# RWKV state of eight decoding samples: four token steps on GpSimd replaced by one chunk of four tokens with TensorE products

## The chip, the core and the metric

The kernel runs on one core of one Trainium2 chip. The metric is the device time of one launch in microseconds; lower is better. Its engines are called PE (TensorE), DVE (VectorE), ACT (ScalarE), POOL (GpSimd) and SP (SyncE) below, as in the profile.

## The reference, cut to what matters

The kernel computes one inference step of a one-layer hybrid decoder: 512 prompt tokens and 8 samples of 4 new tokens each. A combined projection feeds an RWKV-7 mixer and a sparse attention; the two are merged and projected back. The change concerns the RWKV mixer for the samples alone: 8 samples x 16 heads = 128 independent states of 64 x 64, each advanced over 4 tokens.

```python
def step(S, inp):                       # S: (b, h, i, j); i the value index, j the key index
    r_t, k_t, v_t, kk_t, a_t, w_t = inp
    sa = jnp.einsum('bhij,bhj->bhi', S, kk_t)
    S = (S * w_t[:, :, None, :] - sa[..., None] * (kk_t * a_t)[:, :, None, :]
         + v_t[..., None] * k_t[:, :, None, :])
    return S, jnp.einsum('bhij,bhj->bhi', S, r_t)
...
S, o = lax.scan(step, S0.astype(f32), xs)      # 4 steps for a sample
mean = jnp.mean(o, axis=-1, keepdims=True)
var = jnp.mean(jnp.square(o - mean), axis=-1, keepdims=True)
o = (o - mean) * lax.rsqrt(var + GN_EPS) * gn_w.reshape(H, N) + gn_b.reshape(H, N)
o = o + jnp.sum(r * k * r_k, axis=-1, keepdims=True) * v
o = o.reshape(B, T, A_WIDTH) * jax.nn.silu(g.astype(f32))
```

Outputs that depend on it are the sample rows of y and the new state `s_rwkv`.

## The kernel before, in words

**Stages.** The kernel is a sequence of stages: the RWKV mixer of the prompt, the compression of the cached rows, the prompt's attention (`attend_prompt`, here called the prompt stage), the samples' attention, and the output projection. An engine enters a stage when all have ended the one before (`T.enter`, `T.end`).

**The background projection.** All stages up to the samples' attention share one long piece of PE work, the combined projection. Its weights come in halves h of 128 x 1024 numbers: SP loads a half (`w_raw`, L155, two buffers; it waits until `w_lo` of the half two before is made), ACT copies it to a rounded `w_hi` (L161), another engine subtracts to make `w_lo` (L168), and PE multiplies it in four pieces of 12 matmuls each (L200). In the prompt stage `w_lo` is made by POOL; in the others by DVE. Two halves form a chunk, which ACT evacuates (L208). Each engine runs pieces, copies and evacuations in order between its other work, up to a number that a planned place gives (`background(upto)`). The prompt stage holds 12 chunks, 96 pieces. The first 16 stand ahead of PE's entry, the last 12 behind all attention work, and 68 are spread over the rest. At the start of the stage PE and ACT first do some of this background work and then wait to enter.

**The prompt stage.** There are 16 rows (4 groups x 4 heads), each of 4 query tiles t of 128 queries, so 64 units u = 4w + t. PE's work for a unit: two score products S0 and S1 of the next unit (L1919), the transposes T0 and T1 (L1928), and the value product O of the unit before (L1939, L1941). At t = 1 comes the compressed score product C of the next row (L1906), at t = 3 its transpose CT (L1913). DVE reduces scores while it copies them out (`maxes`, L1822; `row_maxes`, L1830), copies T1 (L1870) and combines the outputs (`outs`, L1847 to L1852); ACT takes exponentials (L1756, L1763) and copies T0 (L1796) and CT (L1771). Four PSUM banks serve these jobs in turn, in the order in which `prompt_jobs` lists them: job k takes the bank of job k - 4 and waits until that is copied out (`held`, `taken`).

Ahead of the first row's exponentials ACT has to do all background work up to piece 16: `w_hi` of the halves h0+4, h0+5 and h0+6 and the evacuation of the first two chunks, where h0 is the stage's first half. CT of row 0 waits for these exponentials, and the loop over the units stands behind CT.

**The samples' state.** `rwkv_samples` runs inside the prompt stage. The 128 states lie one to a partition, 64 x 64 numbers each. DVE and ACT make the vectors (`dve_before`, `act_before`); POOL then does `pool_steps`:

```python
for t in range(DEC_T):
    link(tt(prod[:, :, :], S[:, :, :], last_dim(kk, t), ALU.mult))
    tt(S[:, :, :], S[:, :, :], last_dim(w, t), ALU.mult)
    link(row_sums(sa[:, :]))
```

and so on: five products and two sums of 128 x 4096 numbers for a token and two trees of sums (`row_sums`, L1476 and L1478). After each linked instruction `between()` is called, which puts a `w_lo` on POOL where its count is due. POOL's order at the start of the stage is: load the samples' data, `w_lo` of h0+2, wait for the vectors, the first product of 128 x 4096 (L1480), `w_lo` of h0+3 and h0+4.

DVE does five more small operations for the samples in the loop, among them three products of two SBUF tensors (L1521, L1522 and L1524, in units 8, 9 and 11). At the end of the stage DVE and ACT normalise the outputs (`dve_after`, `act_after`), and SP stores the new state (2 MB, L1443) and the outputs (L1445) and waits for both to land before the stage ends (`store`).

Of the kernel before, what the change touches and what calls it, by code (L numbers as in the profile page):

```python
# [19 lines left out]
F32 = mybir.dt.float32  # L20
# [1389 lines left out]
def rwkv_samples(nc, A, ctx):  # L1410

    sb = lambda name, shape: ctx.enter_context(nc.sbuf_tensor(name, shape, F32))
    sem = nc.alloc_semaphore
    X = sb("sx", [P, DEC_T, 6, HD])
    tab = sb("stab", [P, 5, HD])
    S, prod = (sb(n, [P, HD, HD]) for n in ("sS", "s_prod"))  # L1420
    w, kraw, sq, kk, b, k2, rk, o, gate = (
        sb("s_" + n, [P, DEC_T, HD]) for n in ("w", "kraw", "sq", "kk", "b", "k2", "rk", "o", "gate"))
    oc = kraw
    ss, mean, var, bonus = (sb("s_" + n, [P, DEC_T]) for n in ("ss", "mean", "var", "bonus"))
    sa, eps = sb("s_sa", [P, HD]), sb("s_eps", [P, 1])
    loaded, chain, act_done, ready = sem("s_loaded"), sem("s_chain"), sem("s_act_done"), sem("s_ready_in")
    norm_in, var_in, pool_chain, stepped = sem("s_norm_in"), sem("s_var_in"), sem("s_pool_chain"), sem("s_stepped")
    o_done, sent, state_in = sem("s_o_done"), sem("s_sent"), sem("s_state_in")
    last_dim = lambda t, i: t[:, i, None, :].to_broadcast([P, HD, HD])
    over_j = lambda t: t[:, :, None].to_broadcast([P, HD, HD])  # L1430
    over_d = lambda t: t[:, :, None].to_broadcast([P, DEC_T, HD])
    over_t = lambda k: tab[:, None, k, :].to_broadcast([P, DEC_T, HD])
    r, k, v, g, sw, a = (X[:, :, f, :] for f in range(6))

    def load(eng):
        eng.dma_start(X[:, :, :, :], A["smp"].rearrange("h (b t) f -> (h b) (t f)", t=DEC_T)
                      .rearrange("p (t f d) -> p t f d", t=DEC_T, f=6)).then_inc(loaded, 16)
        eng.dma_start(tab[:, :, :], A["stab"]).then_inc(loaded, 16)
        eng.dma_start(S[:, :, :], A["state"]).then_inc(state_in, 16)

    def store(eng):
        eng.wait_ge(stepped, 1)
        eng.dma_start(A["s_rwkv"], S[:, :, :]).then_inc(sent, 16)  # L1443
        eng.wait_ge(o_done, 1)
        eng.dma_start(A["oS"].rearrange("h n d -> (h n d)").rearrange("(p n) -> p n", p=P),  # L1445
                      o[:, :, :].rearrange("p t d -> p (t d)")).then_inc(sent, 16)
        eng.wait_ge(sent, 32)

    def act_before(act):
        f = nc.scalar.activation  # L1450
        act.wait_ge(loaded, 32)
        f(w[:, :, :], sw, ACT.Exp, scale=DECAY_SCALE).then_inc(act_done, 1)
        act.wait_ge(norm_in, 1)
        f(ss[:, :], ss[:, :], ACT.Sqrt).then_inc(act_done, 1)
        f(gate[:, :, :], g, ACT.Sigmoid).then_inc(act_done, 1)

    def act_after(act):
        act.wait_ge(var_in, 1)
        nc.scalar.activation(var[:, :], var[:, :], ACT.Sqrt, bias=eps[:, 0:1], scale=1.0 / HD).then_inc(act_done, 1)

    def pool_steps(pool, between):
        tt = nc.gpsimd.tensor_tensor
        chained = same_engine(pool, pool_chain)
        pool.wait_ge(ready, 1)
        pool.wait_ge(act_done, 1)
        pool.wait_ge(state_in, 16)

        def link(ins):
            chained(ins)
            between()  # L1470

        def row_sums(out):

            n = HD // 2
            while n > 1:
# [1541 lines left out]
```

## Time and profile before

| | us |
|---|---|
| median of three runs | 2391.82 |
| lowest and highest of the three | 2386.79, 2394.43 |
| the profiled execution, own time | 2392.19 |
| span of its trace | 2390.5 |
| PE busy in the span | 2240.8 |
| DVE, ACT, POOL busy | 1238.6, 839.4, 536.7 |

Times in the trace count from the start of the span. Each fp32 matmul of the program appears as two records, and so does each weight load; products of the background are in fp32r and appear as one. A record's duration includes the time in the pipeline, so records overlap, and the rate of a series is read from the start of one to the start of a later one. The prompt stage begins at about 1287.4, when the engines enter, and ends at about 1687.7.

### The profile page before, as it was taken

What the parts mean: (1) busy time and instruction counts of PE and PEld (TensorE: products, weight loads), DVE (VectorE), ACT (ScalarE), POOL (GpSimd) and SP (SyncE); (2) the same over time, 40 slices, a digit from 0 to 9 for tenths busy, and PEclk for the clock granted to TensorE, in tenths of its full rate; (3) what the DMA queues carried; (4) which work ended last, traced back from release to release, by engine and by line L of the source; (5) the groups of instructions that cost most, each with busy time, mean ns of one, the idle gap of its engine ahead of it and who ended that gap; (6) DMA issues with size and microseconds to landing.
All of it is one profiled execution on the core that took longest, in us unless ns stands there. A gap on an engine that the chain in (4) does not pass through costs nothing. (4 is left out here: it accounts for less than half of the span.)

```text
span 2390.5 us, 52200 instructions
## 1 busy us (share of the span) xinstructions
PE 2240.8 (94%) x21478; PEld 2066.5 (86%) x21478; DVE 1238.6 (52%) x2426; ACT 839.4 (35%) x1643; POOL 536.7 (22%) x401
## 2 busy tenths in 40 slices
PE   7999999999999999999998988999889859999997
PEld 6998888888888888999998777888877659999997
DVE  6345555645555553488984454444145415354454
ACT  5333334333333422222222545454222224233342
POOL 0000000000000000011102999999215410000000
PEclk9999999999999999999999999999999879999999
DMA  4222121221212221786765222221859853445564
GB/s 160 92 73 79 51 65 57 64 80 56 74 52 65 73 70 55 256 285 221 254 214 169 64 83 72 77 79 45 296 165 325 281 193 109 135 151 166 185 201 139
DMA packets 142560, 318.88 MB, mean 133 GB/s; under 512 B 27786, under 2 KB 59764, under 8 KB 141300
## 3 DMA queue, kind: packets, MB, share of 16 engines
q1 hardware_dynamic: 102148, 225.64, 28.9%
q0 software_dynamic: 16352, 54.58, 6.8%
q10 hardware_dynamic: 23824, 35.33, 4.5%
q8 instruction: 171, 2.80, 0.5%
q14 instruction: 65, 0.53, 0.1%
HBM read 278.26 MB, written 45.54 MB: 135 GB/s over the span
## 5 line engine op out<-in xcount | busy, mean ns | idle before, releaser
L200 PE MATMUL acc<-xh,w_hi 128*128 128x272 f32 x2944 | 655.9, 304 | 23.7 <-POOL w_lo L168 11.9
L200 PE MATMUL acc<-xh,w_lo 128*128 128x272 f32 x2944 | 614.2, 290 | 0.0
L200 PE MATMUL acc<-xl,w_hi 128*128 128x272 f32 x2944 | 613.7, 290 | 0.0
L200 PEld LDWEIGHTS acc<-xh,w_hi 128*128 128x128 f32 x2944 | 464.2, 191 | 79.9 <-issue 45.4
L200 PEld LDWEIGHTS acc<-xl,w_hi 128*128 128x128 f32 x2944 | 468.9, 191 | 0.0
L200 PEld LDWEIGHTS acc<-xh,w_lo 128*128 128x128 f32 x2944 | 466.2, 191 | 0.0
L168 DVE TENSOR_TENSOR w_lo<-w_raw,w_hi 128x1024 fp32r<-128x1024 f32 x164 | 200.2, 1223 | 207.8 <-ACT w_hi L161 206.0
L161 ACT ACTIVATE w_hi<-w_raw 128x1024 fp32r<-128x1024 f32 x188 | 198.2, 1055 | 294.7 <-PE acc L200 188.7
L2672 DVE TENSOR_TENSOR m_w_lo<-m_w,m_w_hi 128x1024 fp32r<-128x1024 f32 x96 | 117.6, 1225 | 142.1 <-ACT m_w_hi L2607 142.1
L1305 DVE SCALAR_TENSOR_TENSOR b_C<-b_rows,b_pos_s,b_C 128x512 f32<-128x512 f32 x240 | 162.4, 744 | 0.0
L2797 PE MATMUL m_acc<-m_m_hi,m_w_hi 128*128 128x272 f32 x512 | 154.0, 301 | 0.0
L2607 ACT ACTIVATE m_w_hi<-m_w 128x1024 fp32r<-128x1024 f32 x96 | 101.4, 1056 | 135.3 <-PE m_acc L2797 110.7
L2797 PE MATMUL m_acc<-m_m_hi,m_w_lo 128*128 128x272 f32 x512 | 147.8, 289 | 0.0
L2797 PE MATMUL m_acc<-m_m_lo,m_w_hi 128*128 128x272 f32 x512 | 147.3, 288 | 0.0
L1010 PEld LDWEIGHTS rbank<-m 64*64 64x64 f32 x3840 | 120.2, 135 | 22.0 <-issue 14.2
L1010 PE MATMUL rbank<-m 64*64 64x64 f32 x3840 | 132.3, 220 | 0.0
L1756 ACT ACTIVATE a_S<-a_S,a_mx 128x128 f32<-128x128 f32 (+3 forms) x128 | 70.8, 554 | 116.5 <-DVE a_mx L1822 116.4
L2592 POOL DMA_DIRECT2D out_yT<-m_h x8 | 6.1, 756 | 434.9 <-DVE m_h L2721 434.9
L2797 PE MATMUL m_acc<-m_o_hi,m_w_hi 128*128 128x272 f32 x496 | 102.9, 289 | 0.0
L2797 PE MATMUL m_acc<-m_o_lo,m_w_hi 128*128 128x272 f32 x496 | 102.5, 288 | 0.0
L2797 PE MATMUL m_acc<-m_o_hi,m_w_lo 128*128 128x272 f32 x496 | 101.8, 287 | 0.0
L2797 PEld LDWEIGHTS m_acc<-m_m_hi,m_w_hi 128*128 128x128 f32 x512 | 96.4, 188 | 1.2
(422 smaller groups left out, 3482.6 us busy)
## 6 DMA issues: line engine op xcount, KB each, us to landing
w_raw<-in_w_all SPq DMA_DIRECT2D x168, 512.0 KB, 3.5
m_w<-in_w_mo SPq DMA_DIRECT2D x96, 512.0 KB, 3.9
b_rows<-in_cmp_rows SPq DMA_DIRECT2D x128, 256.0 KB, 3.6
w_raw<-in_w_all ACTq DMA_DIRECT2D x20, 512.0 KB, 6.1
tmp_uT<-ub ACTq DMA_DIRECT2D x35, 272.0 KB, 3.2
m_gates<-tmp_uT SPq DMA_DIRECT2D x32, 272.0 KB, 2.7
d_ring<-in_sel_k SPq DMA_DIRECT2D x64, 128.0 KB, 4.5
d_ring<-in_sel_k POOLq DMA_DIRECT2D x64, 128.0 KB, 4.5
```

The source lines that it names most:

```text
L161: self.nc.scalar.activation(self.T.Wh[self.slot(h)][:, :, :], self.T.raw[h % N_RAW][:, :, :], ACT.Copy)\
L168: eng.tensor_tensor(self.T.Wl[self.slot(h)][:, :, :], self.T.raw[h % N_RAW][:, :, :], self.T.Wh[self.slot(h)][:, :, :].bitcast(F32), ALU.s ...
L200: ins = self.nc.tensor.matmul(acc[:, c, 0:HALF], w[:, k % KH, :], x[:, k, c * HALF:(c + 1) * HALF], start=(k == 0 and m == 0), stop=(k == ...
L1010: ins = mm(bank[hp, bank_of[i, name], n * CH:(n + 1) * CH], lhsT(hp, n), rhs(hp, n), start=True, stop=True)
L1305: chained(stt(out=dst(half), in0=src, scalar=w, in1=dst(half), op0=ALU.mult, op1=ALU.add))
L1756: f(S[u % 2][:, k, 0:keys(t)], S[u % 2][:, k, 0:keys(t)], ACT.Exp, scale=-1.0, bias=mx[:, u % 4, k:k + 1], accum_out=sums[:, u % 4, k:k + ...
L2592: pool.dma_start(A["yT"][:, 4 * q:4 * q + 4, cols], h[:, 4 * q:4 * q + 4, cols]).then_inc(sent, 16)
L2607: f(w_hi[x % N_RING_M][:, :, :], w[x % N_RING_M][:, :, :], ACT.Copy).then_inc(w_hi_done, 1)
L2672: v.tensor_tensor(w_lo[j][:, :, :], w[j][:, :, :], w_hi[j][:, :, :].bitcast(F32), ALU.subtract)\
L2797: ins = mm(out[:, c, 0:HALF], a[j][:, k % KW, :], b[:, k, c * HALF:(c + 1) * HALF], start=(start and k == tiles[0] and m == 0), stop=(stop ...
```

## The change

`rwkv_samples` becomes a class `SampleSteps`, whose object `Z` is called at the old places and at new ones. The recurrence over four tokens is written as one chunk. With W the running product of the decays, the eight vectors Q (kk of each token times the decay before it, r times the decay up to it) meet the old state in one product Y; the products of vectors of different tokens are 8 x 8 numbers for a state (`D`); a triangular solve on them gives outputs and corrections (`acc`); the new state is the old one times the total decay plus a sum of eight outer products.

- **State layout.** A partition now holds a key index of half of the heads, and along the partition lie the 64 (head, sample) pairs c of that half and 64 values. The host arranges the input and the output accordingly; the transfers keep their size.
- **PE** gets 12 new jobs in the prompt stage (`SAMPLE_JOBS`), at the end of units 5, 6, 9, 11 and 30, 32, ... 44: VT and YT (16 transposing products of 64 x 64 each), WT (2), Y (128 products with 64 x 64 of the state as weights and 8 columns moving), and U0 to U7 (16 products each with 8 rows, 64 columns of weights and 64 moving). They take part in the turn of the four banks.
- **ACT** copies VT, WT and YT out, **DVE** copies Y and adds each U to its block of the state.
- **POOL** makes the vectors, the dot products and the solve, with instructions of at most 896 numbers in a partition, multiplies the state by the decay (8 of 512), sends keys and values to DRAM and fetches them back with the token on the partition (3 and 8 transfers). Its `w_lo` are no longer set by a count but by a written order, with `w_lo` of h0+2 and h0+3 both ahead of the wait for the vectors.
- **DVE** does the first part of the normalisation in units 24 to 28. The store on SP stays at its place in SP's order.

The diff, cut to its core (the vectors on DVE and ACT differ only by running sums of the decay logarithm, one more exponential and a negated product; the normalisation has the same operations):

```diff
+    def pool_vectors(self, pool, link):
+
+        tt = self.nc.gpsimd.tensor_tensor
+        Q = self.Q8.rearrange("p (t k) d -> p t k d", k=2)
+        pool.wait_ge(self.ready, 1)
+        pool.wait_ge(self.act_done, 2)
+        tt(Q[:, 1:DEC_T, 0, :], self.kk[:, 1:DEC_T, :], self.W[:, 0:DEC_T - 1, :], ALU.mult)
+        link(tt(Q[:, :, 1, :], self.r, self.W[:, :, :], ALU.mult))
+        pool.sem_inc(self.vectors, 1)
+        tt(self.K8[:, 0, :, :], self.k2[:, :, :], self.Ei[:, :, :], ALU.mult)
+        link(tt(self.K8[:, 1, :, :], self.nb[:, :, :], self.Ei[:, :, :], ALU.mult))
+        last = self.W[:, None, DEC_T - 1, :].to_broadcast([P, DEC_T, HD])
+        tt(self.KW[:, 0, :, :], self.K8[:, 0, :, :], last, ALU.mult)
+        link(tt(self.KW[:, 1, :, :], self.K8[:, 1, :, :], last, ALU.mult))
+        pool.dma_start(self.A["s_keys"].rearrange("s p d -> p s d"),
+                       self.KW.rearrange("p k s d -> p (k s) d")).then_inc(self.k_sent, 16)
+
+    def pool_dots(self, link, s):
+
+        tt = self.nc.gpsimd.tensor_tensor
+        n = 7 - 2 * s
+        p = self.prod[:, :, 0:n, :]
+        link(tt(p, self.Q8[:, None, 2 * s + 1:8, :].to_broadcast([P, 2, n, HD]),
+                self.K8[:, :, s, None, :].to_broadcast([P, 2, n, HD]), ALU.mult))
+        m = HD // 2
+        while m > 1:
+            link(tt(p[:, :, :, 0:m], p[:, :, :, 0:m], p[:, :, :, m:2 * m], ALU.add))
+            m //= 2
+        link(tt(self.D[:, :, s, 2 * s + 1:8], p[:, :, :, 0], p[:, :, :, 1], ALU.add))
+
+    def pool_solve(self, link, s):
+
+        tt = self.nc.gpsimd.tensor_tensor
+        n = 7 - 2 * s
+        dst, tmp = self.acc[:, 2 * s + 1:8, :], self.prod[:, 0, 0:n, :]
+        for k, row in enumerate((self.v[:, s, :], self.acc[:, 2 * s, :])):
+            link(tt(tmp, row[:, None, :].to_broadcast([P, n, HD]),
+                    self.D[:, k, s, 2 * s + 1:8, None].to_broadcast([P, n, HD]), ALU.mult))
+            link(tt(dst, dst, tmp, ALU.add))
...
+    def pool_send(self, pool):
+
+        pool.sem_inc(self.solved, 1)
+        keys = self.acc[:, :, :].rearrange("p (t k) d -> p t k d", k=2)[:, :, 0, :]
+        pool.dma_start(self.A["s_values"][0:DEC_T].rearrange("s p d -> p s d"), self.v).then_inc(self.v_sent, 16)
+        pool.dma_start(self.A["s_values"][DEC_T:].rearrange("s p d -> p s d"), keys).then_inc(self.v_sent, 16)
+
+    def pool_fetch(self, pool):
+
+        pool.wait_ge(self.k_sent, 16)
+        pool.wait_ge(self.v_sent, 32)
+        for dst, name in ((self.k_rows, "s_keys"), (self.v_rows, "s_values")):
+            src = self.A[name].rearrange("s (e h g c) d -> s e h g (c d)", e=2, h=2, g=4)
+            for g in range(4):
+                pool.dma_start(dst[32 * g:32 * g + 8, :, :, :, :].rearrange("s e h c d -> s e h (c d)"), src[:, :, :, g, :])\
+                    .then_inc(self.rows_in, 16)
+
+    def pool_decay(self, m):
+
+        block = self.S[:, 8 * m:8 * m + 8, :]
+        self.nc.gpsimd.tensor_tensor(block, block, self.WT[:, 8 * m:8 * m + 8, None].to_broadcast([P, 8, HD]), ALU.mult)\
+            .then_inc(self.decayed, 1)
...
 PROMPT_PIECES, START_PIECES, END_PIECES = PIECES * (PROMPT_CHUNKS - KEY_CHUNKS), 16, 12
-POOL_STEPS = 72
+SAMPLE_JOBS = {5: ("VT", 0), 6: ("WT", 0), 9: ("Y", 0), 11: ("YT", 0), **{30 + 2 * m: ("U", m) for m in range(8)}}
 LOWEST = 1e20
 
 
@@ -1572,8 +1632,11 @@
             order.append(("C" if t == 1 else "CT", w + 1))
         if u:
             order.append(("O", u - 1))
+        if u in SAMPLE_JOBS:
+            order.append(SAMPLE_JOBS[u])
     order.append(("O", NU - 1))
-    engine = {"C": "dve", "S0": "dve", "S1": "dve", "CT": "act", "T0": "act", "T1": "dve", "O": "dve"}
+    engine = {"C": "dve", "S0": "dve", "S1": "dve", "CT": "act", "T0": "act", "T1": "dve", "O": "dve",
+              "VT": "act", "WT": "act", "Y": "dve", "YT": "act", "U": "dve"}
     place, done, out, bank, held = {}, {}, {}, {}, {}
     n, at = {"act": 0, "dve": 0}, START_PIECES
...
-            store_samples(sp)
+            taken(sp, ("U", 7))
+            Z.store(sp)
...
             ins.then_inc(zeroed, 1)
-            lows, steps = [W.h0 + 2], [0]
-            LOWS = W.h_ahead - W.h0 - 2 - END_PIECES // HALF_PIECES - 2
-
-            def between():
-                steps[0] += 1
-                while lows[0] < W.h_ahead and (lows[0] - W.h0 - 4) * POOL_STEPS <= steps[0] * LOWS:
+            link = Z.pool_chained(pool)
+            Z.load(pool)
+            lows = [W.h0 + 2]
+
+            def low(n=1):
+                for _ in range(n):
                     W.low(pool, lows[0])
                     lows[0] += 1
-            load_samples(pool)
-            W.low(pool, lows[0])
-            lows[0] += 1
-            samples_steps(pool, between)
-            while lows[0] < W.h_ahead:
-                W.low(pool, lows[0])
-                lows[0] += 1
+            low(2)
+            Z.pool_vectors(pool, link)
+            low()
+            Z.pool_dots(link, 0)
+            low()
+            Z.pool_dots(link, 1)
+            low()
+            Z.pool_dots(link, 2)
+            Z.pool_dots(link, 3)
+            low(4)
+            taken(pool, ("YT", 0))
+            Z.pool_solve(link, 0)
+            Z.pool_solve(link, 1)
+            low()
+            Z.pool_solve(link, 2)
+            Z.pool_solve(link, 3)
+            Z.pool_send(pool)
+            low()
+            Z.pool_fetch(pool)
+            taken(pool, ("WT", 0))
+            for m in range(4):
+                Z.pool_decay(m)
+            low()
+            for m in range(4, 8):
+                Z.pool_decay(m)
+            low(W.h_ahead - lows[0])
             T.end(pool, W.w_lo, W.h_ahead)
...
+            def sample_out(u):
+                job = SAMPLE_JOBS.get(u, ("", 0))
+                if job[0] == "Y":
+                    dve.wait_ge(pe_jobs, done_at[job])
+                    v.tensor_copy(Z.Y, bank[:, bank_of[job], :].rearrange("p (c v) -> p v c", v=8)).then_inc(ev_dve, 1)
+                if job[0] == "U":
+                    block = Z.S[:, 8 * job[1]:8 * job[1] + 8, :]
+                    dve.wait_ge(Z.decayed, job[1] + 1)
+                    dve.wait_ge(pe_jobs, done_at[job])
+                    v.tensor_tensor(block, bank[:, bank_of[job], :].rearrange("p (c d) -> p c d", d=HD), block, ALU.add)\
+                        .then_inc(ev_dve, 1)
             enter(dve)
             v.memset(tiny[:, :], 1e-30).then_inc(tiny_set, 1)
-            samples_rest = samples_dve(dve)
+            samples_rest = Z.dve_before(dve)
+            norm, norm_rest = Z.dve_norm(dve)
             row_maxes(0)
             maxes(0)
             row_inverse(0)
...
+            H = (slice(0, HD), slice(HD, P))
+
+            def sample_job(name, m):
+                b = job(name, m)
+                if name == "VT":
+                    pe.wait_ge(Z.vectors, 1)
+                    for v in range(8):
+                        for hp in H:
+                            ins = mm(b[hp, v * HD:(v + 1) * HD], Z.Q8[hp, v, :], T.ident[hp, hp], start=True, stop=True)
+                elif name == "WT":
+                    for hp in H:
+                        ins = mm(b[hp, 0:HD], Z.W[hp, DEC_T - 1, :], T.ident[hp, hp], start=True, stop=True)
+                elif name == "Y":
+                    pe.wait_ge(Z.state_in, 16)
+                    taken(pe, ("VT", 0))
+                    for c in range(HD):
+                        for hp in H:
+                            ins = mm(b[hp, 8 * c:8 * c + 8], Z.S[hp, c, :], Z.VT[hp, :, c], start=True, stop=True)
+                elif name == "YT":
+                    taken(pe, ("Y", 0))
+                    for v in range(8):
+                        for hp in H:
+                            ins = mm(b[hp, v * HD:(v + 1) * HD], Z.Y[hp, v, :], T.ident[hp, hp], start=True, stop=True)
+                else:
+                    if m == 0:
+                        pe.wait_ge(Z.rows_in, 16 * 8)
+                    rows = slice(32 * (m % 4), 32 * (m % 4) + 8)
+                    for c in range(8):
+                        for e, hp in enumerate(H):
+                            ins = mm(b[hp, c * HD:(c + 1) * HD], Z.k_rows[rows, e, m // 4, c, :], Z.v_rows[rows, e, m // 4, c, :],
+                                     start=True, stop=True)
+                done(ins)
             background(START_PIECES)
             enter(pe)
             row_scores(0)
```

## Rows read from the trace of the kernel before

**Rows 1.** Windows of the prompt stage: busy of each engine, granted clock, DMA share.
```profile
1287.40:1676.80 389.40, 349.56 (x2617) 309.32 (x2617) 185.25 (x742) 186.84 (x651) 370.38 (x105) 0.96 0.28 82
...
1302.50:1313.40 10.90, 0.03 (x1) 0.00 (x0) 8.66 (x1) 2.24 (x4) 10.82 (x3) 0.73 0.73 186
...
1326.50:1331.00 4.50, 4.46 (x18) 3.59 (x19) 1.22 (x7) 2.85 (x13) 4.42 (x2) 0.50 0.00 0
...
1375.40:1381.30 5.90, 0.07 (x1) 0.00 (x0) 5.87 (x6) 0.36 (x2) 5.82 (x2) 0.54 0.00 0
1381.30:1385.80 4.50, 4.43 (x14) 2.95 (x15) 3.00 (x17) 1.64 (x5) 4.50 (x2) 0.50 0.36 114
1385.80:1657.70 271.90, 255.59 (x1946) 224.54 (x1946) 131.60 (x589) 142.30 (x522) 267.67 (x72) 0.99 0.24 72
...
1491.90:1495.30 3.40, 3.40 (x18) 3.40 (x17) 0.26 (x1) 2.12 (x9) 3.40 (x1) 0.50 0.02 5
```
**Rows 2.** PE's waits from 1287 to 1690: total us, times, longest.
```profile
PE a_bank L1919 <- ACT a_PT L1796: 15.9, 15, 3.0
PE acc L200 <- POOL w_lo L168: 11.9, 2, 10.9
PE a_bank L1919 <- DVE a_PT L1870: 5.9, 1, 5.9
```
**Rows 3.** Timeline at the start of the prompt stage, several engines: start, duration, instruction.
```profile
1302.08 8.81 POOL L1480 TENSOR_TENSOR s_prod<-sS,s_kk 128x4096 f32<-128x4096 f32 x1 [10.01 <-DVEq L1514]
1310.96 2.40 POOL L168 TENSOR_TENSOR w_lo<-w_raw,w_hi 128x1024 fp32r<-128x1024 f32 x1
...
1310.78 1.06 ACT L161 ACTIVATE w_hi<-w_raw 128x1024 fp32r<-128x1024 f32 x1 [7.34 <-DMA w_raw<-in_w_all]
...
1322.79 1.06 ACT L161 ACTIVATE w_hi<-w_raw 128x1024 fp32r<-128x1024 f32 x1 [0.47 <-ACT ub L208]
...
1326.54 0.48 PE L1913 MATMUL a_bank<-ident,a_Sc 128*128 128x128 f32 x1 [3.57 <-ACT a_Sc L1763]
```
**Rows 4.** Median time from issue to landing of the weight loads.
```profile
w_raw<-in_w_all SPq DMA_DIRECT2D x168, 512.0 KB, 3.5
```
**Rows 5.** DVE's groups, 1322 to 1670: busy, mean ns.
```profile
L1852 DVE SCALAR_TENSOR_TENSOR a_out<-a_bank,a_coef,a_part 128x64 f32<-128x64 f32 x64 | 18.2, 284 | 2.3
...
L1522 DVE TENSOR_TENSOR s_rk<-s_rk,stab 128x256 f32<-128x256 f32 x1 | 6.8, 6848 | 0.0
...
L1534 DVE TENSOR_TENSOR s_kraw<-s_o,s_mean 128x256 f32<-128x256 f32 x1 | 0.4, 428 | 0.0
```
**Rows 6.** Timeline of PE, series of small products; x counts records.
```profile
145.97 1.15 PE L1010 MATMUL rbank<-KR,BK 64*64 64x64 f32 x32
146.95 1.10 PE L1010 MATMUL rbank<-BK,KR 64*64 64x64 f32 x32
...
168.37 0.92 PE L1052 MATMUL rbank<-UV,G 64*64 64x64 f32 x26
...
1334.37 1.08 PE L1906 MATMUL a_bank<-a_kcT,a_q 64*128 64x32 f32 x8
...
1771.22 0.27 PE L2359 MATMUL d_bank<-d_kN,d_q 128*32 128x4 f32 x4
```
**Rows 7.** POOL's groups in the stage: busy, mean ns.
```profile
L168 POOL TENSOR_TENSOR w_lo<-w_raw,w_hi 128x1024 fp32r<-128x1024 f32 x24 | 57.2, 2384 | 3.8 <-ACT w_hi L161 2.2
...
L1476 POOL TENSOR_TENSOR s_prod<-s_prod 128x512 f32<-128x512 f32 x8 | 10.3, 1293 | 0.5
```
**Rows 8.** Windows of the stage before, around two short series of small products.
```profile
1020.00:1022.00 2.00, 0.41 (x5) 0.22 (x5) 1.71 (x5) 0.62 (x1) 0.00 (x0) 1.00 0.98 315
1022.00:1024.30 2.30, 2.30 (x18) 1.85 (x18) 2.30 (x4) 1.16 (x2) 0.00 (x0) 0.99 0.66 253
1024.30:1027.70 3.40, 3.40 (x17) 3.40 (x17) 3.40 (x6) 0.38 (x1) 0.00 (x0) 0.50 0.72 220
```
**Rows 9.** Timeline of PE near the end of the stage.
```profile
1664.75 0.52 PE L200 MATMUL acc<-xh,w_hi 128*128 128x272 f32 x2 [1.03 <-POOL w_lo L168]
```

More of the change, by code:

```diff
@@ L1544, in rwkv_samples, with dve_norm, first_sum, last_sum @@
-    return load, store, act_before, act_after, pool_steps, dve_before, dve_after, o_done
+    def dve_norm(self, dve):
+        vv = self.nc.vector
+        tt = vv.tensor_tensor
+        link = same_engine(dve, self.chain)
+        oc, sq, mean, var = self.kraw, self.sq, self.mean, self.var
+        def first_sum():
+            dve.wait_ge(self.solved, 1)
+            link(vv.reduce_sum(mean[:, :], self.outs, axis=AX.X))
+        def last_sum():
+            link(vv.reduce_sum(var[:, :], sq[:, :, :], axis=AX.X))
+            dve.sem_inc(self.var_in, 1)
+        def rest():
+            dve.wait_ge(self.act_done, 5)
+            link(vv.reciprocal(var[:, :], var[:, :]))
+            link(tt(oc[:, :, :], oc[:, :, :], self.over_d(var), ALU.mult))
+            link(tt(oc[:, :, :], oc[:, :, :], self.over_t(3), ALU.mult))
+            link(tt(oc[:, :, :], oc[:, :, :], self.over_t(4), ALU.add))
+            link(tt(oc[:, :, :], oc[:, :, :], self.rk[:, :, :], ALU.add))
+            tt(self.o[:, :, :], oc[:, :, :], self.gate[:, :, :], ALU.mult).then_inc(self.o_done, 1)
+        return [first_sum,
+                lambda: link(vv.tensor_scalar(mean[:, :], mean[:, :], 1.0 / HD, None, ALU.mult)),
+                lambda: link(tt(oc[:, :, :], self.outs, self.over_d(mean), ALU.subtract)),
+                lambda: link(tt(sq[:, :, :], oc[:, :, :], oc[:, :, :], ALU.mult)),
+                last_sum], rest
@@ L1772, in row_turned, with sample_copy @@
                     .then_inc(ev_act, 1)
+            def sample_copy(u):
+                if u not in SAMPLE_JOBS or SAMPLE_JOBS[u][0] not in ("VT", "WT", "YT"):
+                    return
+                job = SAMPLE_JOBS[u]
+                dst = {"VT": Z.VT[:, :, :], "WT": Z.WT[:, :], "YT": Z.acc[:, :, :]}[job[0]]
+                src = bank[:, bank_of[job], 0:HD if job[0] == "WT" else 8 * HD]
+                act.wait_ge(pe_jobs, done_at[job])
+                f(dst, src if job[0] == "WT" else src.rearrange("p (v d) -> p v d", d=HD), ACT.Copy).then_inc(ev_act, 1)
             background(4)
@@ L1866, in _ @@
                     samples_rest.pop(0)()
+                if u >= 24 and norm:
+                    norm.pop(0)()
                 dve.wait_ge(exp_done, 2 * u + 2)
```

218 lines of the change are left out of this document (99 added, 119 removed).

## Prediction

> **What bounds the kernel now.** I read the page first, then windows over the prompt stage, PE's waits in it, the timelines around the longest ones, and last the rows that price the new work. The whole change lies in the prompt stage, so only its length counts. The window over the stage [rows 1] shows PE busy for 349.6 of 389.4 us and POOL for 370.4. POOL looks like the fuller engine, but an engine bounds a stage only where others wait for it: of PE's waits [rows 2] only 11.9 us are for POOL, in two places, and 15.9 us are for ACT's copy of T0 at the row boundaries (15 of them, 1.06 us each). For the rest PE works. So the stage is as long as PE's work plus a few gaps. Taking some 270 us of arithmetic off POOL (370 less the 100 worked out below) gives nothing by itself; what it gives is in the gaps, and what PE is given instead is paid in full wherever it doesn't fall into one.
>
> **Gaps that the old steps made.** (1) The start. POOL waits until 1302.08 for the samples' vectors, then multiplies for 8.8 us, and only then makes `w_lo` of h0+3 at 1310.96 [rows 3]; PE stands still for 10.9 us [rows 1, 2]. Then PE does its four pieces, at half clock at first, and waits again, until CT can start at 1326.54, for ACT's exponentials [rows 3]. (2) A lock between POOL and DVE. DVE's product of two SBUF tensors L1522 takes 6.85 us where one like it without POOL beside it takes 0.43, while `a_out`, which has one input in PSUM, keeps to 0.28 in all 64 units though POOL multiplies all the time [rows 5]. PE waited 5.9 us behind it [rows 2], and the granted clock was 0.50, the 1.2 GHz level, for the next 4.5 us of work after this pause [rows 1]. (3) Near the end, a `w_lo` that came 1.0 us late.
>
> **The sum, step by step.**
>
> *PE's new products.* VT, YT: 16 fp32 products each, Y 128, U 8 x 16, WT 2: 290 products, 580 records. VT and YT have the exact form of the L1010 series, 64 x 64 in the two diagonal quarters: 32 records from 145.97 to 146.95, 0.98 us or 31 ns a record [rows 6]. Together 2.0, and WT 0.1. For U the nearest is L1052, where two products in turn share their rows and differ in output half, as in U: 26 records in 0.92 with 0.22 of tail, 28 ns [rows 6]. U has 8 rows instead of 64 but the same 64 columns on both sides; I take 0.98 us a job, 7.8 for eight. Y has 64 x 64 weights as in L1010 but 8 moving columns. Below 31 ns I have no row; above, L1906 with 128 columns of weights and no change of quarter takes 1.08 us for 8 records, 116 ns with the tail taken off, half of it for half the columns is 58 (an estimate), and L2359 with 4 moving columns takes at most 0.27/4 = 68 [rows 6]. I take 31 since the weights and the change of quarter are L1010's and the short moving side cannot lengthen it: 7.8, with 7 and 17 as ends. Sum **+17.7**.
>
> The Trainium skill (TensorE: Matmul & The Clock Gate, Part 3: Packing small matmuls, The mechanism) says that weight loads overlap with running products only where the row group differs. By that rule U, whose pairs share a row group, would run its loads and products one after the other. L1052 shows 28 ns in that very arrangement, so the trace does not agree for 64 rows; no row shows it for 8. The rule's result is a rival below.
>
> *The start.* Now `w_lo` of h0+2 and h0+3 both stand ahead of POOL's wait, and PE runs its four pieces on from 1302.4, ending at about 1308.4. It then waits for CT, which hangs on ACT: `w_hi` of h0+4 still comes at 1310.78, when its load has landed [rows 3]; POOL's `w_lo` of it ends 2.4 later [rows 7], at about 1314.3; the load of h0+6 may then start and lands 3.5 later [rows 4]; `w_hi` at 1318 instead of 1322.79. The evacuation that held it back before is done by then. CT comes as much earlier: **-4.8**. So of the 10.9 us only this is gained; the rest becomes the wait for CT. The half clock after it, 4.5 us as now [rows 1], stays.
>
> *The lock.* POOL's new instructions hold at most 896 numbers; 512 take 1.29 us and a `w_lo` 2.38 [rows 7]. At units 8 to 11 POOL mostly waits for `w_hi`. DVE can be held 2.4 us at most, which it bears. That boundary still waits its 1.06: 5.9 - 1.06 = **-4.8**, and the half clock of 4.5 us behind it, in which half is lost, **-2.2**. The late `w_lo` at the end **-1.0** [rows 9].
>
> *What U fills.* U0, U2, U4, U6 stand at the end of units 30, 34, 38, 42, just where PE waits 1.06 us for T0's copy; 4 x 0.98 = **-3.9**. The longest of these waits, 3.0 us [rows 2], is at unit 30, and the clock was at 0.50 for 3.4 us soon after [rows 1], which cost 1.7; with one of the three us filled I put half of that, **-0.8**. The other eight jobs fill nothing: in the window 1385.8 to 1657.7 PE is idle 16.3 us, hardly more than the boundary waits.
>
> *The clock under Y.* Y is 7.8 us in which PE moves 8 columns a product. The windows in [rows 8] show the clock at 2.4 GHz and then at 1.2 from 1024.3 on, though PE was busy for the 2.3 us ahead of that; before it lay a pause and two series of small products. I therefore expect the clock to fall within Y. Its second half then takes up to twice as long (+2.7), and the half clock lasts some 4.5 us of ordinary work behind it, as after the pause at 1375 [rows 1], at half loss (+2.3): **+5.0**, with 0 and 7 as ends.
>
> *At no cost.* ACT's three copies and DVE's nine more operations lie in units in which both wait for PE. POOL: 24 `w_lo` at 2.38 are 57 us, the new arithmetic some 45 by [rows 7], in 389; its last duty for U is due at unit 30, and its order ties it to `w_hi` of h0+12, made at about unit 23, which leaves some 5 units of 5.3 us less 15 us of work. Its 11 small transfers and SP's order move nothing; the state is stored at the same place. The end of the stage hangs, as before, on PE's last piece, ACT's evacuation and square root, DVE's last six operations and the two stores. If the cover on POOL were gone, each us that U0 waits would count.
>
> Sum: 17.7 - 4.8 - 4.8 - 2.2 - 1.0 - 3.9 - 0.8 + 5.0 = +5.2. On the profiled execution's 2392.2 that is 2397.4; it ran 0.4 above the median of the three, so the forecast is **2397**.
>
> **Rivals.** *A, the clock holds under Y.* Products come every 31 ns, without a pause. Against it: [rows 8]. Time 2392, no change. Chance 0.20.
> *B, products of one row strip do not overlap* (the rule of the skill). U takes twice as long, +7.8, of which nothing is filled: 2405, slower. Against it: L1052. Chance 0.08.
> *C, Y's weight loads are not hidden behind 8 columns.* At 58 ns Y takes 14.8: +7, 2404. For it: nothing shows such a short moving side under 64 columns of weights; against it: loads of different quarters. 0.08.
> *D, U0 waits for POOL.* The fetch, the decay and the solves are one chain with `w_lo`s between; if it is 15 us slower than I count, PE stands about 8 us at unit 30: 2405. 0.06.
> *E, faster.* The load of h0+6 and the exponentials are not what CT waits for once PE is no longer late, so that CT comes within 2 us of PE's last early piece, at 1311. Then 15 us instead of 4.8 are gained and no half clock follows (another 2.2): 2385. It decides from 12 us on. Against it: the load of h0+4 lands at 1310.8 whatever POOL does [rows 3]. 0.08.
>
> **How the numbers follow.** The forecast's case has 0.42, with its own range 2392 to 2402; 0.08 is left for what I don't see, on both sides. About 0.3%, 7 us, is what a measurement of this kernel can tell from no change: 2385 and 2399 are the bounds. Slower: B, C, D and 0.3 of the forecast's case, 0.35. Faster: E and a little, 0.10. Same 0.55. The range 2386 to 2407 takes in A, B, C and D, and leaves out E and the far ends of Y.
>
> **What would show it.** After the change: POOL's long rows gone and its busy time in the stage near 100 us; no wait of PE for `w_lo`, but one of about 12 us ahead of CT at 1308, CT at about 1322; no DVE product over 3 us; Y as one series of 256 records, 8 to 12 us, and a window at 0.50 in or behind it; U jobs of 1.0 us, those of units 30, 34, 38, 42 in place of the boundary waits; the end of the loop 5 us later than 1657.7. The prediction is wrong if CT comes before 1315, if Y or U run above 40 ns a record at full clock, or if PE waits at U0.

## The result, and the profile after

The changed kernel takes **2399.88 us** (median of 10 runs, 2396.61 to 2405.50), the kernel before 2390.61 (10 runs, 2386.40 to 2395.95): a ratio of **1.0042**, 95% interval 1.0032 to 1.0052, slower by 9 to 10 us. The forecast was 2397. The profiled execution took 2398.52, its span is 2396.6; against the profiled one of before that is +6.3, of which the sum had +5.2.

The page's first row after the change (busy us, share of the span, records of each engine):

```profile
PE 2258.7 (94%) x22058; PEld 2083.9 (87%) x22058; DVE 1229.3 (51%) x2440; ACT 840.9 (35%) x1647; POOL 268.5 (11%) x394
```

POOL's 536.7 us have halved and PE has 580 records more, as counted. Windows of the stage (busy of each engine, granted clock, DMA share, GB/s); they answer to [rows 1]:

```profile
1287.40:1693.90 406.50, 380.06 (x3278) 339.31 (x3277) 178.38 (x761) 191.26 (x659) 101.97 (x97) 0.96 0.30 90
...
1313.40:1321.69 8.29, 0.00 (x0) 0.00 (x0) 0.00 (x0) 4.06 (x12) 7.74 (x9) 0.50 0.26 97
1321.69:1327.50 5.81, 5.81 (x23) 4.28 (x23) 1.22 (x7) 2.83 (x13) 5.26 (x9) 0.51 0.34 93
...
1372.90:1375.20 2.30, 2.30 (x81) 2.30 (x80) 0.91 (x3) 0.00 (x0) 0.00 (x0) 1.00 0.02 7
1375.20:1384.75 9.55, 9.55 (x185) 9.53 (x182) 0.00 (x0) 0.00 (x0) 0.00 (x0) 0.50 0.01 2
1384.75:1388.80 4.05, 4.05 (x15) 2.55 (x14) 2.50 (x7) 1.23 (x3) 0.00 (x0) 0.50 0.01 4
1389.80:1661.00 271.20, 259.72 (x2189) 228.17 (x2188) 140.38 (x598) 141.90 (x522) 57.91 (x48) 0.99 0.26 74
```

The three windows from 1372.90 are Y and what follows it: some 80 records in 2.3 us at 2.4 GHz, then the clock falls to 1.2 GHz while PE is busy without a pause, the rest of Y runs at 53 ns a record, and ordinary work still runs at half clock until 1388.8. PE's waits in the stage, beside [rows 2]:

```profile
PE a_bank L2021 <- ACT a_Sc L1845: 12.4, 1, 12.4
PE a_bank L2027 <- ACT a_PT L1887: 11.8, 13, 1.9
PE a_bank L2036 <- DVE a_out L1944: 1.3, 7, 0.2
PE a_bank L2036 <- ACT s_wt L1863: 0.9, 1, 0.9
```

No wait for POOL is left. The 5.9 us behind DVE have gone too, and there are fewer boundary waits. The wait ahead of CT has grown from 3.6 to 12.4 us, which was forecast, and a new one of 0.9 us, for the copy of WT, was not. The start of the stage, with the rows that answer to [rows 3] (start, duration, instruction):

```profile
1303.02 0.60 POOL L1549 TENSOR_TENSOR s_k_rows<-s_kk,s_w 128x192 f32<-128x192 f32 x1 [9.13 <-DVEq L1497]
...
1307.96 0.96 PE L2014 MATMUL a_bank<-a_kcT,a_q 64*128 64x32 f32 x7
...
1310.84 1.06 ACT L161 ACTIVATE w_hi<-w_raw 128x1024 fp32r<-128x1024 f32 x1 [7.01 <-DMA w_raw<-in_w_all]
...
1317.94 1.06 ACT L161 ACTIVATE w_hi<-w_raw 128x1024 fp32r<-128x1024 f32 x1 [4.17 <-DMA w_raw<-in_w_all]
...
1321.69 0.47 PE L2021 MATMUL a_bank<-ident,a_Sc 128*128 128x128 f32 x1 [12.36 <-ACT a_Sc L1845]
```

PE's new series (x counts records):

```profile
1351.42 1.15 PE L2059 MATMUL a_bank<-ident,s_k_rows 64*64 64x64 f32 x32
...
1356.93 0.33 PE L2062 MATMUL a_bank<-ident,s_w 64*64 64x64 f32 x4
1357.82 0.49 PE L2027 MATMUL a_bank<-a_kT,a_q 64*128 64x128 f32 x4 [0.56 <-ACT a_PT L1887]
...
1359.84 0.66 PE L2036 MATMUL a_bank<-ident,a_S 128*128 128x128 f32 x4 [0.94 <-ACT s_wt L1863]
...
1372.88 11.92 PE L2068 MATMUL a_bank<-s_vt,sS 64*64 64x8 f32 x256
1384.73 2.08 PE L2027 MATMUL a_bank<-a_kT,a_q 64*128 64x512 f32 x4
...
1517.47 1.15 PE L2080 MATMUL a_bank<-s_v_rows,s_k_rows 8*64 8x64 f32 x32
1518.70 0.49 PE L2027 MATMUL a_bank<-a_kT,a_q 64*128 64x128 f32 x4
```

VT and U each hold PE for 1.08 us, from their first record to the next job's. At 1518.70 no wait stands behind U: it has taken the boundary's.

**Four units at a time.** CT stands once in every four units, so the distance from one CT to the next measures what these four units (a group) cost, wherever the whole has shifted. Worked out from the timelines of the profiled executions (us; "start" is from PE's first background piece behind the stage before, about 288 records ahead of C, to the first CT; the numbers are CT to CT, first to last):

```
               start |  1    2    3    4    5    6    7    8    9   10   11   12   13   14   15 | sum 1-15
before          54.3 | 17.9 19.7 26.8 20.8 19.7 19.7 20.9 24.5 20.1 20.1 19.4 21.3 19.7 19.9 18.4 | 308.9
after           50.0 | 18.3 21.8 32.2 21.9 19.7 19.7 22.5 22.8 20.9 20.8 20.6 22.3 19.7 19.7 18.4 | 321.4
before, again   54.0 | 17.4 19.7 27.7 20.9 19.7 19.7 22.4 25.4 23.0 19.7 19.4 21.3 19.7 19.8 18.4 | 314.1
after, again    49.9 | 18.5 21.8 32.4 21.9 19.7 19.7 22.5 22.8 20.8 20.8 20.6 22.3 19.7 19.7 18.4 | 321.7
```

Group 2 holds VT and WT, 3 Y, 4 YT, 8 U0, 9 to 11 two U each, 12 the last. An undisturbed group takes 19.7. The whole span's +6.1 is: -0.5 ahead of that first piece, -4.3 at the start, +12.5 in the groups, -1.9 from the last CT to the next stage, +0.3 behind it.

### The profile page after: what moved, and what is told of

It reads as the page before. It is cut to its first block and busy times, and to the rows that moved or that the text cites. A ratio compares the mean times of both kernels' runs of the same rounds, so it can differ in the third digit from the quotient of the medians.

```text
span 2396.6 us, 53390 instructions
## 1 busy us (share of the span) xinstructions
PE 2258.7 (94%) x22058; PEld 2083.9 (87%) x22058; DVE 1229.3 (51%) x2440; ACT 840.9 (35%) x1647; POOL 268.5 (11%) x394
## 5 line engine op out<-in xcount | busy, mean ns | idle before, releaser
L2939 PEld LDWEIGHTS m_acc<-m_m_lo,m_w_hi 128*128 128x128 f32 x512 | 96.3, 188 | 1.2
```

What stands on the lines that cost most here:

```text
L2939: ins = mm(out[:, c, 0:HALF], a[j][:, k % KW, :], b[:, k, c * HALF:(c + 1) * HALF], start=(start and k == tiles[0] and m == 0), stop=(stop ...
```

## The experiments

Each kernel ran 11 or 12 times (the changed one again 5 times) beside the kernel before on the same chip; ratios are to the kernel before in the same comparison, with 95% intervals. A difference "by the medians" from the changed kernel is taken from its 2399.88 above, which was measured in another comparison, so differences of 1 to 4 us by the medians alone show little; the groups of the profiles carry the readings.

**1. The start alone.** Kernel before:

```diff
-            W.low(pool, lows[0])
-            lows[0] += 1
+            for _ in range(2):
+                W.low(pool, lows[0])
+                lows[0] += 1
             samples_steps(pool, between)
```

> The kernel before, with one edit: POOL makes w_lo of h0+2 and of h0+3 both ahead of its wait for the samples' vectors, as the changed kernel does; the four steps stay on POOL. Theory (start term of the prediction): PE does its four early pieces without the 10.9 us gap and then waits for CT, which comes 4.8 us earlier; nothing else moves: -4.8 us, a ratio to before of 0.998. Rival 1: CT comes when it came before, because POOL's lock and load order hold the load of h0+6 as long: 0, ratio 1.000. Rival 2: the w_lo of h0+4 now stands behind POOL's long multiply and comes later: +3 us, ratio 1.001.

2387.52 us, ratio 0.9991 (0.9979 to 1.0003); the interval takes in no change. In the profile the start is 50.2 us instead of 54.3, with one wait of 12.5 ahead of CT: the term of the start is right. But group 3 grew from 26.8 to 30.1. DVE's first product now meets POOL elsewhere:

```profile
1362.48 7.60 DVE L1521 TENSOR_TENSOR s_rk<-sx,s_k 128x256 f32<-128x256 f32 x1
...
1370.52 0.69 PE L1929 MATMUL a_bank<-ident,a_S 128*128 128x128 f32 x2 [2.68 <-DVE a_PT L1871]
...
1372.22 6.83 DVE L1522 TENSOR_TENSOR s_rk<-s_rk,stab 128x256 f32<-128x256 f32 x1
```

In the kernel before that product took 4.12 us, which its units could bear; 7.60 make PE wait 2.7. How long DVE is held (the lock) hangs on where the two engines meet; the gain at the start was partly lost to it.

**2. The lock alone.** Kernel before, DVE's four products of two SBUF tensors in the loop made memsets, so that the bonus term and the gate are left out (two of the four lines):

```diff
-        return [lambda: link(tt(rk[:, :, :], r, k2[:, :, :], ALU.mult)),
+        return [lambda: link(vv.memset(rk[:, :, :], 1.0)),
...
-            link(tt(gate[:, :, :], gate[:, :, :], g, ALU.mult))
+            link(vv.memset(gate[:, :, :], 1.0))
```

> The kernel before, but DVE's four products of two SBUF tensors in the loop (three for s_rk, one for s_gate) are replaced by memsets of the same tensors; so the bonus term and the gate are left out of the samples' result. Theory (lock term of the prediction): the 6.85 us product and PE's 5.9 us wait behind it go, and the half clock behind the pause with them: -4.8 and -2.2, together -7.0 us, ratio 0.997. Rival: the granted clock falls at that place anyway (in the trace of before it falls at 1375.8, the wait begins at 1375.5, so the wait may not be its cause): -4.8 us alone or less, ratio 0.998, and the window behind 1376 still shows 0.50.

2387.09 us, ratio 0.9990 (0.9978 to 1.0002); this interval takes in no change too. Group 3 falls from 26.8 to 19.3, so the lock and its half clock were worth 7.5 there, and the rival falls: at that place the clock stays at 2.4 GHz.

```profile
1374.30:1378.80 4.50, 4.50 (x35) 3.67 (x34) 3.39 (x13) 1.52 (x4) 4.50 (x1) 1.00 0.08 19
```

Group 4 grows from 20.8 to 23.4, since a wait comes up that the pause had covered: ACT makes the next `w_hi` when its load lands, behind POOL's multiplying, and copies T0 after that:

```profile
1385.65 1.06 ACT L161 ACTIVATE w_hi<-w_raw 128x1024 fp32r<-128x1024 f32 x1 [3.09 <-DMA w_raw<-in_w_all]
...
1387.24 0.70 PE L1919 MATMUL a_bank<-a_kT,a_q 64*128 64x256 f32 x4 [2.54 <-ACT a_PT L1796]
```

Net -4.9 in the two groups, -4.5 by the medians, some -2.4 by the ratio. In the changed kernel POOL is free at that time and group 4 has no such wait (21.9 is 20.8 and YT's 1.1).

**3. Y nearly left out.** Changed kernel, with 8 of the 64 columns:

```diff
-                    for c in range(HD):
+                    for c in range(8):
```

> The changed kernel with 8 of Y's 64 columns of state products (16 of 128 products; 224 of 256 records left out), all else as it is. In the changed kernel Y ran 2.6 us at full clock (40 records a us, 25 ns each) and the rest at half (23 a us), 11.9 us in all, and the half clock ended at 1388.8. Theory: 224 records x 25 ns = 5.6 us of work and the whole fall of the clock with it (5.4 us inside Y, 2 us behind) go: -13 us against the changed kernel, ratio to before 0.9987. The prediction's own terms say -11.8: ratio 0.9993. Rival: the clock falls at 1375 anyway, as in the kernel before, and costs 3 to 5 us of the ordinary work there: -6 to -9 us, ratio 1.001 to 1.002.

2386.64 us, ratio 0.9985 (0.9973 to 0.9997), 13.2 below the changed kernel. Group 3 takes 21.0 instead of 32.2, so 7/8 of Y and its clock are 11.2. The expectation's 25 ns a record was my misreading: it counted rows of windows of 1 us, in which a record across an edge counts in both. From record to record Y runs at 29.5 ns at 2.4 GHz (64 records in 1.89 us) and 53.3 at 1.2 GHz, so the 224 records left out are 6.6 at full clock and the rest is the clock. The fall did not vanish altogether. One of 3.4 us stayed at 1374.0, and another stands at 1421.8, in group 5 (21.6, was 19.7):

```profile
1374.00:1377.40 3.40, 3.40 (x16) 2.71 (x12) 1.95 (x7) 1.52 (x4) 0.00 (x0) 0.50 0.00 0
```

**4. Y in eight parts.** Changed kernel; first at the end of units 7 to 14, YT at 15:

```diff
-SAMPLE_JOBS = {5: ("VT", 0), 6: ("WT", 0), 9: ("Y", 0), 11: ("YT", 0), ...
+SAMPLE_JOBS = {5: ("VT", 0), 6: ("WT", 0), **{7 + m: ("Y", m) for m in range(8)}, 15: ("YT", 0), ...
...
-                    for c in range(HD):
+                    for c in range(8 * m, 8 * m + 8):
```

> The changed kernel with Y cut into 8 parts of 16 products, at the end of units 7 to 14, and YT at the end of unit 15: the same products, each part 32 records. Theory (the clock is what Y costs beyond its work): no window at 0.50 near 1375, parts of 0.9 us, and the two parts at the end of units 10 and 14 stand in a boundary wait: -7.5 us and -1.6 us against the changed kernel, ratio to before about 1.0004. Rival 1 (the price is the products', through weight loads that do not hide behind 8 columns): nothing is gained, ratio 1.004. Rival 2: YT later makes U0 wait for POOL: no gain or a loss, with a wait of PE at U0.

2395.85 us, ratio 1.0017 (1.0005 to 1.0030), -4.0 by the medians. Less than expected: in place of one fall of 13.7 us there are three of 3.4. One, at 1361.8, stands ahead of the first part, just behind the wait that WT left (it ended at 1361.07). The other two begin right behind the parts of units 9 and 13, whose last records start at 1378.62 and 1402.73. The next expectation puts them beside the boundary waits of units 10 and 14, and that is wrong: the parts of those units start only at 1384.81 and 1408.89.

```profile
1361.80:1365.20 3.40, 3.40 (x18) 3.40 (x17) 0.66 (x1) 1.46 (x4) 0.00 (x0) 0.50 0.00 0
1378.90:1382.30 3.40, 3.40 (x11) 1.90 (x12) 1.74 (x6) 0.81 (x3) 0.00 (x0) 0.50 0.00 0
1402.80:1406.20 3.40, 3.40 (x16) 1.87 (x13) 1.56 (x5) 0.48 (x1) 0.00 (x0) 0.50 0.00 0
```

Then off the boundaries (the parts of units 9 and 13 stay), at units 7, 8, 9, 11, 12, 13, 15, 16, YT at 17:

> The changed kernel with Y in 8 parts again, but at the end of units 7, 8, 9, 11, 12, 13, 15, 16 and YT at unit 17: no part stands next to the boundary wait that follows units 10 and 14. With parts beside those waits (units 7 to 14) the trace showed three falls of 3.4 us, two of them (1378.9, 1402.8) right behind a part and its boundary, in place of one of 13.7 us. Theory: a part lowers the clock only where a wait adjoins it, so without that there is no fall from 1365 to 1410 and the whole 7.5 us come back: -7.5 us against the changed kernel, ratio to before 1.001. Rival: a part anywhere lowers it, or the phase decides: falls remain, -3 to -4 us as with units 7 to 14, ratio 1.0025.

2396.45 us, ratio 1.0020 (1.0007 to 1.0033). In this profile the clock stays at 2.4 GHz all the way:

```profile
1361.00:1490.00 129.00, 121.57 (x1170) 107.38 (x1168) 68.92 (x284) 63.29 (x227) 39.01 (x40) 1.00 0.28 74
...
1364.46 1.10 PE L2070 MATMUL a_bank<-s_vt,sS 64*64 64x8 f32 x32
```

Groups 3 to 6 take 88.7 instead of 93.5, -4.8 (90.8 with the first order); -3.4 by the medians. The 7.5 expected stood on the same misreading of 25 ns, and each part adds its own tail (0.9 us of records, 1.03 to the next job). What Y loses to the clock is 5 us, and nearly that came back.

That the place beside a wait is what matters is not shown. The parts of units 9 and 13, behind which the clock fell before, stood in this order too and no fall came; by the medians the two orders are alike; and experiment 8, with the same places, has a fall of 3.4 us at 1396.7, right behind the part of unit 13 (last record at 1395.89), with no wait of PE between 1379 and 1401:

```profile
1396.70:1400.10 3.40, 3.40 (x16) 2.69 (x12) 1.39 (x5) 1.52 (x4) 0.00 (x0) 0.50 0.00 0
```

What holds in every profile is the length: with Y in one block the clock fell 1.9 to 2.5 us after its first record and stayed down for 13.7 us (five profiles); with Y in parts no fall between 1360 and 1420 was longer than 3.4 us (three profiles).

**5. U nearly left out, and U at the boundaries.** Changed kernel, two edits, each by itself:

```diff
-                    for c in range(8):
+                    for c in range(1):
                         for e, hp in enumerate(H):
```

> The changed kernel with one of eight column groups in each U (2 of 16 products; 7/8 of the rank 8 update left out). Theory: 7/8 of eight times 1.08 us is 7.6, but four of the jobs stand in boundary waits which come back when they go, 4 x 0.95 = 3.8: -3.8 us against the changed kernel, ratio to before 1.0026. Rival: nothing is filled and U costs its whole length: -7.6, ratio 1.001.

2397.67 us, ratio 1.0025 (1.0013 to 1.0037): -2.2 by the medians. Groups 9 to 11 lose 0.6, 0.6 and 0.8 each, where two U shrink by about 0.95 each. The boundary waits come back (0.6 to 0.8 us at the ends of units 34, 38 and 42, and 2.6 instead of 1.8 at unit 30), so filling is shown and the rival falls.

```diff
-... **{30 + 2 * m: ("U", m) for m in range(8)}}
+... **{30 + 4 * m: ("U", m) for m in range(8)}}
```

> The changed kernel with its eight U jobs at units 30, 34, 38, ... 58, all in front of a boundary wait, instead of 30, 32, ... 44 (four of eight there). Theory (filling): four more boundary waits of 1.06 us take up a U of 1.08 us: -4.2 us against the changed kernel, ratio to before 1.0025. Rival: a U beside the wait lowers the clock, as parts of Y did, each fall 3.4 us at half clock, 1.7 us lost: anything from -4.2 to +2 us, with new windows at 0.50 behind units 34 to 58.

2398.75 us, ratio 1.0030 (1.0016 to 1.0043): -1.1. Groups 9 to 11 take 19.8, 19.8 and 19.5, each 1.0 or 1.1 less than with two U. Boundary waits are fewer and the last group has none to fill (18.4 becomes 19.5); the rival takes another part, a fall of 3.4 us at 1583.2 behind the U of unit 46 (group 12: 23.4, was 22.3). A fall at 1501.3, behind U0, makes group 8 24.4 instead of 22.8, though up to there the order is that of the changed kernel. PE's boundary waits in this run:

```profile
PE a_bank L2027 <- ACT a_PT L1887: 10.0, 12, 2.1
```

**6. What CT waits for.** Changed kernel, ACT's order:

```diff
             def background(upto):
+                upto = upto if opened else min(upto, 8)
...
+                opened.append(u)
                 background(place["T1", u])
```

> The changed kernel with one order changed on ACT: until unit 0 is done it makes no more w_hi than h0+4, so the exponentials of row 0 no longer stand behind w_hi of h0+6, whose load lands at about 1317.9. PE needs h0+5 only some four units later. Theory (the 12.4 us wait ahead of CT is ACT's order): ACT reaches the exponentials at 1312.2, CT comes at about 1315 instead of 1321.7 (-6.8), and less half clock behind it (0 to -2): -7 to -9 us against the changed kernel, ratio to before 1.0005 to 1.001. Rival (rival E's counterpart: what was ahead of CT comes back as a wait for w_lo or w_hi of h0+5, h0+6 within the first units): CT early, but PE waits again before unit 4, gain below 3 us.

2393.39 us, ratio 1.0011 (1.0000 to 1.0022), -6.5: the start takes 43.1 instead of 50.0, and no wait for a weight follows in its place up to 1345. (Later in this one execution the clock stood at 1.2 GHz twice for 6.8 us, at 1468.9 and 1492.8, which took 5 of the 7 back. This execution lies only 0.8 us above the median of the twelve, and at their mean granted clock of 0.974, so nothing shows that the others are without it.)

```profile
PE a_bank L2023 <- ACT a_Sc L1846: 5.4, 1, 5.4
PE a_bank L2029 <- ACT a_PT L1888: 0.9, 1, 0.9
PE a_bank L2038 <- DVE a_out L1946: 0.2, 1, 0.2
```

The same edit in the kernel before:

> The kernel before with ACT's order changed alone, as in the last one: the exponentials of row 0 ahead of w_hi h0+5 and h0+6. In the kernel before PE waits for CT only 3.6 us, since POOL's late w_lo of h0+3 holds it for 10.9 us before. Theory: the 3.6 us and a little of the half clock go: -3.6 to -4.6 us, ratio 0.998 to 0.9985; so that the same edit is worth 3 us more in the changed kernel. Rival: w_lo of h0+4, which POOL makes behind its 8.8 us of multiplying, is what PE waits for next: nothing gained, ratio 1.000.

2389.76 us, ratio 1.0002 (0.9991 to 1.0013): no change, but not for the rival's reason. CT still waits 3.0 us, and ACT waits for DVE:

```profile
1328.74 1.28 ACT L1764 ACT_TABLE_LOAD   x1 [10.91 <-DVE a_cmx L1832]
```

There PE reaches C so late that C, DVE's maxima, the table load and the exponentials are the path, 4.4 us in a row, which ACT's order only shadowed. Two chains ended together; the expectation had seen one.

**7. Both kernels again,** unedited:

> The changed kernel once more, unedited, for a second profile and more times beside before. The two profiled executions so far differ by 6.3 us, the medians by 9.3. Theory: the profiled executions are single draws from times that scatter by 3 us either way with the place at which the granted clock falls; over new runs the ratio stays 1.004 (1.0032 to 1.0052) and the new profile differs from the first only in where and how long the clock is at 0.50, with rows of units of the same lengths elsewhere. Rival: the first profile missed a wait that most executions have; the new one shows it.

> The kernel before once more, unedited, for a second profile. Theory: ratio 1.000; the row of units with the lock is again 7 us longer than the undisturbed 19.7 us (it was 26.8), the start again waits 10.9 and 3.6 us. Rival: the lock is a matter of where DVE's product meets POOL's, and costs a different sum in another execution (2 to 4 us), which would explain why leaving out DVE's products gave 4.5 us by the medians and not 7.0.

Changed: 2399.14 us (5 runs), ratio 1.0040 (1.0027 to 1.0053). Its groups equal the first's within 0.2 us (table above); only stretches outside this stage differ. The first profile missed nothing. Before: 2393.65 us, ratio **1.0014** (1.0003 to 1.0025) to itself. So 3 us between two medians is within what this measurement does with one kernel. Much of it goes with the granted clock: among the other executions of the kernel before (33, 34 and 29 in the three comparisons) a mean clock higher by 0.001 went with 1.1 to 1.7 us less (correlation -0.7 to -0.8), and these eleven had 0.9724 on the mean where the 29 beside them had 0.9738. Its group 3 took 27.7, its start 54.0, with waits of 11.2, 5.0 and 3.6: the same lock, a little dearer, so the rival (2 to 4 us) has nothing for it in this profile.

**8. The three orders together,** on the changed kernel: Y in parts off the boundaries, U at 30, 34 to 58, ACT's order:

> The changed kernel with three orders changed together: Y in 8 parts at the end of units 7, 8, 9, 11, 12, 13, 15, 16 with YT at 17 (3.4 us by the medians when alone), U at units 30, 34, ... 58 (1.1 us alone), and ACT's exponentials of row 0 ahead of w_hi h0+5 and h0+6 (6.5 us alone). If the three add up: -11 us against the changed kernel, ratio to before 0.9996 (0.998 to 1.001). Rival: the three share one effect, the half clock, and give 7 to 8 us together: ratio 1.001.

**2383.76 us, ratio 0.9981 (0.9969 to 0.9992)**: 15.4 below the changed kernel in the same comparison, and 4 to 6 below the kernel before, not far above the 3 us by which that kernel differed from itself. In its profiled execution, at 2392.80 one of the slowest of its twelve, the start takes 42.7 and the groups 319.4, together 9.3 less than after; so the profile bears out most of the sum of 11, but not the 15. The profiled execution had a granted clock of 0.973, ten of the other eleven 0.975 to 0.980, so part of the 15 is clock time that this profile does not show; why they had it stays open.

## Why the prediction was right, point by point

**The start, -4.8:** -4.3 in the profiled pair, with CT at 1321.69 where about 1322 was given, and held by what was named: ACT, behind the load of h0+6 (`w_hi` at 1317.94, 1318 forecast). Experiment 6 shows that cause by removing it. Rival E is refuted as stated; an order on ACT would make most of its 10 us true (-6.9 at the start in experiment 6).

**The lock, -4.8 and -2.2:** group 3 had 7.1 us above 19.7, and experiment 2 took 7.5 off. What the sum did not see is that a pause covers later waits. This did no harm here, since POOL's multiplying, which made the covered wait, went as well. DVE's products beside POOL kept to the bound of 2.4 us:

```profile
L1535 DVE TENSOR_SCALAR s_mean<-s_mean 128x4 f32<-128x4 f32 x1 | 2.1, 2075 | 0.0
L1504 DVE TENSOR_TENSOR s_rk<-sx,s_k 128x256 f32<-128x256 f32 x1 | 1.7, 1676 | 0.0
```

**PE's products, 17.7:** 31 ns a record was forecast. Y ran at 29.5 at full clock, 7.6 us (7.8 forecast); VT and U have 0.93 us from first to last record, 30 ns, and hold PE for 1.08, so U is 8.6 for 7.8 and VT and YT 2.2 for 2.0. Rivals B and C are refuted: neither 8 rows nor 8 columns make a record dearer. By the rule of the Trainium skill (TensorE: Matmul & The Clock Gate, Part 3: Packing small matmuls, The mechanism) the weight loads of U's pairs, in one row group, would not overlap with running products; their 30 ns is that of VT, whose pairs change the row group, so the trace does not agree.

**WT, 0.1, ACT's copies at nothing:** this is the term that failed, by 1.0. Group 2 grew by 2.1, VT is 1.1 of it. Jobs use four banks in turn, and T1 of unit 7, four jobs behind WT, waited 0.9 us for ACT's copy of WT from its bank. WT ended at about 1357.3, but in ACT's order its copy stands behind the exponentials of the next row's C, which come in the same unit:

```profile
1358.95 0.31 ACT L1845 ACTIVATE a_Sc<-a_Sc,a_cmx 128x32 f32<-128x32 f32 x1
...
1359.59 0.20 ACT L1863 ACTIVATE s_wt<-a_bank 128x64 f32<-128x64 f32 x1
```

So a job of 0.3 us cost its place in the rotation and in ACT's order, not only its length. No run moved WT, so this rests on the wait in the traces (0.9 us in the profiles of the changed kernel and of its variants).

**What U fills, -3.9 and -0.8:** U0 left 1.8 of the 3.0 us; behind U2, U4 and U6 0.1 us or nothing was left. Groups 8 to 12 grew by 2.0, of which -1.7 is the fall at 1491.9 that before had and after has not; 3.7 remains, with 3.9 forecast (7.8 - 3.9). The -0.8 for that fall is not borne out as a cause: all five profiles of the kernel before and its variants have a fall there, but so have five of the eight with a full U0 (at 1492.4 in the second order of experiment 4, at 1501.3 with U at the boundaries). Its absence in this pair is the draw, and the fall at 1474.2, which after has and before has not, cancels it.

**Y and the clock, +5.0:** Y held PE for 11.85, group 3 was 12.5 above 19.7. Less 7.6 for the products, the clock took 4.9. That this is the 5.0 of the sum is in part luck: within Y the loss was 4.3 and not 2.7, since the clock fell after 2.3 us and not halfway, and behind Y it was 0.6 and not 2.3. Rival A is refuted by both profiles of the changed kernel, and by the parts, which gave nearly 5 back. That the block is the cause is shown: the same products in parts brought no such fall in three profiles. What exactly in a series of small products lowers the clock is not shown.

**Late `w_lo`, -1.0:** the stretch behind the last CT is 1.9 shorter.

**Rival D:** no wait at U0 for POOL; POOL's arithmetic and weights came to 102 us, 100 forecast.

So the steps give what the profiled pair shows, +6.1 of span for +5.2: above the sum lie WT (+1.0), the start (+0.5), VT and YT (+0.2), group 1 (+0.4) and a fall at 1474.2 in group 7 (+1.6), which the kernel before had too in its second execution (1468.2); below it groups 8 to 12 (-1.1), the tail of the stage (-0.9), group 3 (-0.4: -0.1 lock, -0.2 Y, -0.1 its clock), group 14 (-0.2), and what lies ahead of the stage and behind it (-0.2). That the medians differ by 9 to 10 and the profiled pair by 6 is not explained by a wait: before's profiled execution was 1.6 above the median of its ten, after's 1.4 below, and the kernel before, repeated, moved by as much. Where within 6 to 10 us the true step lies stays open; the range held it with room, but by the medians the step is nearly twice the 5.2 of the sum.

## What to carry to other kernels

Work taken off an engine is worth what others waited for it, here 4 + 7 + 2 us for some 270 of arithmetic; cost each gap with what comes second behind it, and look for two chains that end at the same moment. Put small products between large ones: 128 of them in one block cost 5 us in clock, in eight parts there were at most two falls of 3.4 us behind them, each worth about half its length; in front of a wait a series of 1 us was nearly free, if the clock held. A short job in a rotation of banks costs its place there and in the order of the engine that empties the bank, and small orders around a change (the three edits of experiment 8) gave back more than the change cost.

## What the runs showed of the hardware that was not expected

- The granted clock fell while PE was busy without any pause: 1.9 to 2.5 us into 256 records with 8 moving columns, in all five profiles that have them in one block, each time for 13.7 us; at 1.2 GHz a record takes 53.3 ns instead of 29.5. Behind a series of only 32 it fell in some executions for 3.4 us, without a wait beside it too (1396.7 in experiment 8).
- A DVE product of 128 x 256 from two SBUF inputs beside POOL's took 4.12, 5.35, 6.83, 6.85 or 7.60 us, by where it met POOL's instruction; one at the end of the stage, without POOL beside it, 0.43.
- One kernel measured against itself gave 1.0014, interval 1.0003 to 1.0025: an interval from a single set of runs is too narrow for steps of 3 us.
